# VectorE's conditioning group first in the batches that two engines share

## The reference

```python
cond = jax.nn.silu(c)
for l in range(DEPTH):
    mod = (cond @ w_ada[l] + b_ada[l])[:, None, :]
    sh1, sc1, g1, sh2, sc2, g2 = jnp.split(mod, 6, axis=-1)
    h = rms_norm(x) * (1.0 + sc1) + sh1
    z = h @ w_in[l]
...
    mix = jnp.concatenate([out_a, out_b, out_c], axis=-1) @ w_out[l]
    x = x + g1 * mix
    h = rms_norm(x) * (1.0 + sc2) + sh2
    x = x + g2 * conv_ffn(h, ffn_w_up[l], ffn_conv_w[l], ffn_conv_b[l], ffn_w_down[l])
```

## Time and profile before

| | us |
|---|---|
| median of the 3 runs | 2469.16 |
| profiled execution, its own time | 2469.46 |
| its span, first to last instruction | 2467.3 |
| TensorE (PE) matmuls busy | 2374.0 (96%) |
| VectorE (DVE) busy | 1850.6 (75%) |
| ScalarE (ACT) busy | 1144.2 (46%) |
| GpSimd (POOL) busy | 298.1 (12%) |
| DMA, mean over the span | 242 GB/s |

### The profile page before, as it was taken

One profiled execution on the slowest core, in us unless ns is written; L12 is line 12 of the kernel. 1 busy time (PEld: TensorE's weight loads), 2 busy tenths in 40 slices (PEclk: granted clock), 3 DMA queues, 4 the chain that ended last, 5 costly groups with the idle time before them and its releaser, 6 DMA issues.

```text
span 2467.3 us, 38202 instructions
## 1 busy us (share of the span) xinstructions
PE 2374.0 (96%) x15360; PEld 2052.5 (83%) x15360; DVE 1850.6 (75%) x2555; ACT 1144.2 (46%) x1613; POOL 298.1 (12%) x433
## 2 busy tenths in 40 slices
PE   6889999989999999999999999998999999999999
PEld 2568888878888888888887899888888888888888
DVE  2447876779998889888987676666999667766775
ACT  2233654345554455445444366535545345544553
POOL 3331321230101000110031121001010000000000
PEclk8899998999999999999999999999999999999999
DMA  8988886777989888988887877555797566555664
GB/s 294 340 285 273 265 275 213 240 259 249 295 282 324 281 259 261 296 294 257 257 273 240 259 228 229 179 163 161 251 293 236 189 189 190 187 194 189 189 192 147
DMA packets 450512, 596.90 MB, mean 242 GB/s; under 512 B 24172, under 2 KB 397984, under 8 KB 450080
## 3 DMA queue, kind: packets, MB, share of 16 engines
q1 hardware_dynamic: 394640, 392.47, 49.3%
q0 software_dynamic: 55296, 201.35, 25.2%
q10 hardware_dynamic: 400, 0.65, 0.1%
HBM read 592.30 MB, written 2.10 MB: 241 GB/s over the span
## 4 chain that ended last, share of the span: by engine, by line
PE 78%; DVE 11%; issue 4%; DMA 3%; ACT 3%; POOL 0%; ACTq 0%; DVEq 0%
PE bank L1090 78%; DVE wlo L1663 3%; DMA ada<-in_w_ada_dram 3%; DVE acc L1657 2%; ACT whi L1416 2%; DVE T L1682 1%; DMA rows<-in_b_ada_dram 0%; DVE r L1731 0%; ACT sc_s L1537 0%; DVE T L1746 0%; DVE yg L1689 0%; ACT hx L1484 0%; DVE yv L1689 0%; DVE hx L1767 0%; DVE mx L1699 0%
## 5 line engine op out<-in xcount | busy, mean ns | idle before, releaser
L1090 PE MATMUL bank<-hx,whi 128*128 128x512 f32 (+1 forms) x4480 | 1363.5, 364 | 6.4 <-DVE hx L1891 3.0
L1663 DVE TENSOR_TENSOR wlo<-raw,whi 128x1024 fp32r<-128x1024 f32 (+2 forms) x774 | 910.4, 1181 | 456.2 <-ACT whi L1416 454.5
L1416 ACT ACTIVATE whi<-raw 128x1024 fp32r<-128x1024 f32 (+2 forms) x774 | 781.0, 1018 | 828.6 <-PE bank L1090 775.0
L1090 PE MATMUL bank<-hx,wlo 128*128 128x256 f32 x3840 | 1089.7, 284 | 27.7 <-DVE hx L1767 19.4
L1090 PEld LDWEIGHTS bank<-hx,whi 128*128 128x128 f32 x4480 | 804.1, 190 | 150.1 <-issue 11.9
L1090 PEld LDWEIGHTS bank<-hx,wlo 128*128 128x128 f32 x3840 | 732.7, 191 | 45.8 <-issue 20.3
L1090 PE MATMUL bank<-mx,whi 128*128 128x512 f32 (+1 forms) x2096 | 617.9, 359 | 1.5 <-DVE xT L1713 1.5
L1090 PE MATMUL bank<-mx,wlo 128*128 128x256 f32 x1728 | 489.4, 283 | 0.0
L1090 PEld LDWEIGHTS bank<-mx,whi 128*128 128x128 f32 x2096 | 375.2, 192 | 66.0 <-issue 9.3
L1059 POOL DMA_DIRECT2D ada<-in_w_ada_dram x384 | 236.2, 617 | 1489.4 <-DVE acc L1657 913.8
L1090 PEld LDWEIGHTS bank<-mx,wlo 128*128 128x128 f32 x1728 | 331.1, 192 | 1.8 <-issue 1.2
(11 more groups left out here) (163 smaller groups left out, 1272.5 us busy)
## 6 DMA issues: line engine op xcount, KB each, us to landing
ada<-in_w_ada_dram POOLq DMA_DIRECT2D x384, 512.0 KB, 5.9
raw<-in_ffn_w_up_dram SPq DMA_DIRECT2D x352, 512.0 KB, 4.6
raw<-in_ffn_w_down_dram SPq DMA_DIRECT2D x176, 512.0 KB, 4.4
raw<-in_w_in_dram SPq DMA_DIRECT2D x128, 512.0 KB, 5.2
raw<-in_w_out_dram SPq DMA_DIRECT2D x48, 512.0 KB, 4.9
raw<-in_w_out_dram SPq DMA_DIRECT2D x32, 256.0 KB, 4.2
raw<-in_mla_w_uq_dram SPq DMA_DIRECT2D x12, 384.0 KB, 3.6
raw<-in_mla_w_ukv_dram SPq DMA_DIRECT2D x6, 512.0 KB, 5.7
```

The lines of the kernel that those rows point to most:

```text
L1090: return pe.matmul(out_, lhsT, rhs, start=start, stop=stop, skip_group_check=True)
L1416: return act.activation(out_, in_, ACT.Copy)
L1663: i_ = tt(dst, src, high.bitcast(F32), ALU.subtract)
```

## The change

The ring of a shared batch becomes 4, 0, 5, 1, 6, 2, 7, 3, so that it ends with TensorE's T3. The burst of group 3 places `acopy` and the turn (one slot later), in place of `asum`. A burst waits for the turn of the batch before only where the ring's next group is group 0 of a batch, which in a shared batch is no longer its first.

```diff
+def mixed_batch(b):
+    return 2 * b not in VECTOR_HALVES and 2 * b + 1 in VECTOR_HALVES
+
+
 def ring_order(b):
 
-    if 2 * b not in VECTOR_HALVES and 2 * b + 1 in VECTOR_HALVES:
-        return [8 * b + 4 * (x % 2) + x // 2 for x in range(8)]
+    if mixed_batch(b):
+        return [8 * b + 4 * (1 - x % 2) + x // 2 for x in range(8)]
     return list(range(8 * b, 8 * b + 8))
...
-        if g % 8 == 7:
+        if g % 8 == (3 if mixed_batch(g // 8) else 7):
             self.add("acopy", g // 8)
             self.turns.append([1, g // 8])
         self.ada_g += 1
...
             self.add("asum", b, d)
-            if d == 1:
+            if d == 1 and not mixed_batch(b):
                 self.add("acopy", b)
                 self.turns.append([TURN_LAG, b])
...
-        elif self.ada_debt >= 1 and not self.sums and not (self.ada_g % 8 == 0 and (had or self.turns)):
+        elif self.ada_debt >= 1 and not self.sums and not (RING[self.ada_g] % 8 == 0 and (had or self.turns)):
             self.ada_debt -= 1
             self.burst()
```

## The result

The changed kernel takes 2455.45 us (median of 11 runs, 2450.17 to 2460.11) against 2468.5 for the kernel before (11 runs, 2461.83 to 2471.68): ratio 0.995, interval 0.9943 to 0.9958, 0.5% faster. Its profiled execution took 2455.01 us with a span of 2452.9.

The account below looks back on a forecast made before the run. TensorE was taken as the bound, with only 39 us lacking a matmul in the two attention stretches. A to G summed to -0.7 us from 2469.46 profiled; 2468.7 was forecast, no measurable change, range 2463 to 2474.5.

Parts of the forecast that it names:

- A: Batch 4's last burst, layer 0: its wait for a load behind GpSimd's first sum of squares goes, -3.4 us.
- B: Layer 0's transition to feed-forward: the wait for GpSimd's last sum of squares goes, 8.81 to 7.41 us, -1.4 us.
- C: Batch 3's last burst and its sum over partitions fall into layer 0's half-clock stretch and cost more, +1.8 us.
- D: Layer 0, inverse behind unit 35: a VectorE part in slot 36 lengthens TensorE's wait, +0.6 us.
- E: Waits for rotated queries: two parts now ahead in layer 0, one leaves in layer 1, +0.2 us.
- F: Transition ahead of layer 1: its burst moves to where TensorE is bound, the root's wait goes, +1.2 us.
- G: The rest: one first burst of a layer 0 batch waits for loads, other moved parts stay hidden, +0.3 us.
- Rival 1: Half-clock stretches in both layers shorten or go, a dense burst breaking layer 0's: 2463 us, chance 0.18.
- Rival 2: Batch 4's stall moves to its second or third burst, so the gain there is lost: 2472 us, chance 0.15.
- Rivals 3 and 4: 3: long half-clock fall behind layer 0's rotation, 2476, chance 0.1; 4: TensorE next waits for raw weights, 2473.5, chance 0.07.

Follow-up runs that it names:

- e4: The kernel before with the new order in batch 2 alone: 2460.68 us, ratio 0.9972.
- e3: The kernel before with the new order in batches 2 and 3 alone: 2457.93 us, ratio 0.9957.
- e6: The kernel before, old order, with sum over partitions and turn one slot earlier in batches 2, 3 and 4: 2461.38 us, ratio 0.9974.
- e0: The kernel before, unchanged, run again: 2467.88 us, ratio 0.9998.
- e2: The kernel before with the new order in batches 9 and 10 alone, all in layer 1: 2467.81 us, ratio 1.0.
- e13: The kernel before, old order, with no burst placed in the transition ahead of layer 1: 2465.85 us, ratio 0.9989.
- e12: The kernel before, old order, with slot 68 left without a part: 2468.98 us, ratio 1.0004.
- e11: The changed kernel, but batch 3's last burst may not come before slot 86: 2459.95 us, ratio 0.9965 to the kernel before.
- e5: The kernel before with the new order in batch 3 alone: 2460.87 us, ratio 0.9979.
- e14: The changed kernel with slots 36 and 425 left without a part: 2454.98 us, ratio 0.9943 to the kernel before.
- e8: The changed kernel as it is, run again: 2455.09 us, ratio 0.9948 to the kernel before.
- e9: The changed kernel with the old order in batch 10: 2458.99 us, ratio 0.9954 to the kernel before.
- e10: The changed kernel with the old order in batch 9: 2458.21 us, ratio 0.9958 to the kernel before.
- e1: The kernel before with the new order in batch 4 alone: 2464.59 us, ratio 0.9987.

## Why the prediction was wrong

The new places, slot by slot, came out as the prediction lists them. (Of the old ones it has batch 10's last part and its turn one slot early: they stand in 479 and 484.)

- **A, -3.4:** right, -3.6 measured. The reason given, the load behind the first sum of squares, is 1.6 to 2.1 of it; distance and time to landing are the rest (e4). Its place was not tied to the order in batch 4 (e3, e6).
- **B, -1.4:** the length came, 7.41 us in both profiles of the change, but the size is luck and the cause given is wrong. In four profiles with the old layer 0 (before, e0, e2, e13) the wait was 1.88 us, none, 1.46 and 0.71, and the transition took 8.80, 7.41, 8.38 and 7.64: the mean gain is 0.65 us. The rest of the stretch's -1.7 is time at half clock, 1.1 and 5.4 us before and 1.4 after. And VectorE's late parts don't set the wait: e12 has parts in slots 106 to 109 and no wait, e11's last part is in 105 and the wait is 2.88 us.
- **C, +1.8:** the cost came out by luck, and the net did not. The burst took 3.31 us and the sum over partitions 1.08, against 1.93 and 0.64: 1.8 more, as forecast.
```profile
418.55 1.08 PE L1094 MATMUL bank<-acc,onez 128*32 128x256 f32 x8
419.40 3.31 PE L1094 MATMUL bank<-ada,condz 128*32 128x256 f32 x32
```
  But the fall ends at 422.2, so the burst's last 0.5 us ran at full clock. This is the stretch of the burst, its mean granted clock 0.57:
```profile
419.40:422.70 3.30, 3.30 (x37) 1.41 (x29) 0.00 (x0) 0.00 (x0) 1.26 (x3) 0.57 0.23 29
```
  In the 2.80 us at half clock it did what takes 1.93 - 0.51 = 1.42 us at full clock, which is 1.97 times. In e5, where 3.22 of the burst's 3.49 us lie in the fall, the same working gives 1.94. The prediction's 1.69 for a quarter is too low for a whole burst. The Trainium skill (TensorE: Matmul & The Clock Gate, part 1) gives the half clock as 4 of 8 pulses; an estimate from that is twice the time, and the trace agrees with 1.97. What hid it is that the fall ended inside the burst. It was also 3.4 us shorter than before, worth 1.7, and the net was -0.3.
- **D, +0.6:** right, TensorE's wait grew by 0.44. With part 36 away that goes (e14). The rest of the stretch's +1.4 is mostly time at half clock, 3.2 and 1.2 us before and 4.3 and 3.5 after, worth 0.9.
- **E, +0.2:** -0.2. Layer 0's wait stayed 1.68 us with two parts ahead of it; layer 1's fell from 1.91 to 1.68 as forecast. No fall of the clock came in layer 0.
- **F, +1.2: this step failed, "so I add nothing for the clock".** The transition itself went as worked out (+1.1 net, root without its wait). But the clock changed with it: in five of seven profiles without the burst the fall near 1400 us does not come, and in the changed kernel's two the one in the transition begins 3.4 us ahead of the first product, in idle time, or is 3.4 us long instead of 6.8. e13 has the step alone at -2.7 (-0.5 to -4.9), 3.9 us from the forecast. No step at all priced layer 1's largest change, the fall near 1595 us, 13.7 us before and 6.8 in both profiles of the change. It is 6.8 or 10.2 us in the four profiles with the changed layer 1 (the changed kernel, e2, e8, e11) and 13.7 in all others, e9, e10, e13 and e14 among them. Why is open; that one slot left free (e14) brings it back says how little is needed.
- **G, +0.3: this step failed too, in sign and size.** "Moves of 3 or 4 slots in the attention of layer 0" were held to be covered. They ended or shortened four waits instead (by 1.2 and 1.6 near 282 in the two profiles, 0.9 and 0.4, 0.5 and 1.0, and 1.25 between 357 and 381), some 4 us, and added one of 0.8 to 1.45 (T1 of batch 3, the tight burst that G looked for at T0). I had priced what a moved part might newly uncover and had not listed the waits of the kernel before that were already uncovered, 0.5 to 1.3 us each, with a part or a burst next to them.
- **Rival 1** (clock, 0.18) was the nearest, and its clock terms came: 1.7 in layer 0, and no fall behind layer 1's rotation (though e0, without the change, had none either). Its reason, a dense burst breaking the fall, fell with e11. The rule of the Trainium skill (TensorE: Matmul & The Clock Gate, part 1) that activity releases the throttle spoke for it; here one burst more or less in the fall made no difference (10.2 us with it and without). The rival left out the long fall near 1595 us. **Rival 2** came at another burst (T1 of batch 3, 0.8 to 1.45). **Rivals 3 and 4** did not come.

The sum with measured sizes: -3.6 (A) - 1.7 (B, its clock included) - 0.3 (C, its shorter fall included) + 0.4 (D) - 0.2 (E) - 2.7 (F by e13) is -8.1 and leaves 5 of the 13 for G's waits and layer 1's remaining clock. What stays open: what shortens the falls of either layer, what makes GpSimd's last sum late, and how much of layer 1's 4 us is real.

## What to carry to other kernels

When work is moved between slots, first list every wait of the engine that sets the pace, down to half a microsecond, in the stretches that it leaves and enters: a move can end such waits as well as make them, and here that was worth about as much as the one large wait that caught the eye. Put filler of the waiting engine itself (a burst) in front of the matmuls that wait: a burst of 1.93 us took up the whole wait of 1.68 us in e3 and e6. Keep filler of the engine that feeds them (VectorE's parts) from following one another, as near 282 us. Compare traces between the same two matmuls, with moved work taken out, and compare two profiles of each kernel before a difference of 2 us is believed.

## What the runs showed of the hardware that was not expected

- The granted clock carried some 8 to 10 of the 13 us, by estimates from the profiles (8.3, and 10.0 by the wider set) and the timed runs (9). Taking TensorE's filler out of a wait, and paying for it elsewhere, made the kernel faster (e13, 0.9989, up to 0.9998), and its profile had 5 us less at half clock behind it.
- A short group of instructions understates what half clock costs. A quarter of a burst, 8 matmuls of 128 x 32 by 128 x 256, was recorded with 1.08 us at 1.2 GHz and 0.64 at 2.4, 1.69 times; a whole burst of 32 did its work 1.97 times as slowly while the clock was at half (1.94 in e5). (A burst is 16 products in the code, recorded as 32 matmuls; the 64 given ahead of the prediction is wrong.)
- One slot's difference in where a load is issued moved a wait from 3.4 to 4.9 us (e12). Four slots between issue and use hid it in e1, where the load landed in 4.8 us, but left 0.98 us in e11, where it took 7.0.
